# Sixteen activation rows per tensor, moved from a 1280-byte pitch to pitches of 1264 and 1272 bytes

## The reference

```
mod = silu(c) @ w_ada + b_ada                      # shift, scale, gate, twice
h   = rmsnorm(x) * (1 + scale1) + shift1
qa, ka, va, qb, kb, vb, r, glr = split(h @ w_in)   # 2048 -> 6160
oa  = attention, 16 heads of 64, three dilations, shared bias
ob  = gated linear attention, 4 heads, dk 128, dv 256
x   = x + gate1 * (concat(norm(oa), norm(ob) * silu(r)) @ w_out)
h2  = rmsnorm(x) * (1 + scale2) + shift2
g, u = split(h2 @ w_up)                            # 2048 -> 2 * 5632
x   = x + gate2 * ((silu(causal_conv3(g)) * u) @ w_down)
```

## Time and profile before

| | |
|---|---|
| median of 3 runs | 1544.93 us (1543.18 to 1546.24) |
| the profiled execution's span | 1544.0 us |
| mean granted TensorE clock | 0.993 of 2.4 GHz |
| busy: TensorE matmuls, weight loads | 98%, 89% |
| busy: VectorE, ScalarE, GpSimd | 57%, 41%, 3% |
| DMA | 371 MB, 240 GB/s on average |

### The profile page before, as it was taken

The page is one execution under the profiler, slowest core; times in us unless marked ns, Lnnn a source line. Parts: engine busy times, 40 slices in busy tenths (PEclk is TensorE's granted clock), DMA queues, the critical chain, the costliest instruction groups (busy, mean ns, idle before and its releaser), DMA issues.

```text
span 1544.0 us, 27862 instructions
## 1 busy us (share of the span) xinstructions
PE 1514.8 (98%) x11762; PEld 1372.8 (89%) x11762; DVE 875.7 (57%) x1509; ACT 633.9 (41%) x873; POOL 52.4 (3%) x89
## 2 busy tenths in 40 slices
PE   8999999999999889999999999999999999999999
PEld 4877888888888557768899999999999999999999
DVE  3655676666667435557454555555554565656574
ACT  3433444434445215235333333334333445545453
POOL 2000000001111000000000000000000000000000
PEclk8999999999999999999999999999999999999999
DMA  9998777777777997997644444454545444454541
GB/s 354 400 355 346 307 257 257 257 259 267 255 288 270 413 414 309 422 363 292 251 164 164 164 164 169 159 184 147 188 146 182 163 172 178 166 181 172 178 176 53
DMA packets 62283, 370.98 MB, mean 240 GB/s; under 512 B 7431, under 2 KB 7913, under 8 KB 27081
## 3 DMA queue, kind: packets, MB, share of 16 engines
q1 hardware_dynamic: 56096, 351.08, 60.6%
q0 software_dynamic: 5904, 17.93, 3.4%
q10 hardware_dynamic: 162, 0.22, 0.0%
HBM read 359.32 MB, written 9.88 MB: 239 GB/s over the span
## 4 chain that ended last, share of the span: by engine, by line
PE 89%; DMA 5%; DVE 3%; SPq 2%; ACT 1%; issue 1%; POOL 0%; ACTq 0%; DVEq 0%
PE ps L989 26%; PE ps L990 25%; PE ps L991 25%; PE ps L941 4%; PE ps L934 1%; SPq L710 1%; DMA ring<-in_w_ada_early 1%; DMA ring<-in_w_out 1%; DMA ring<-in_cache_k_win 1%; DMA proj<-in_tables 1%; ACT whi L1501 1%; DVE wlo L2028 1%; PE ps L1321 1%; DMA ring<-in_w_ada 1%; PE ps L1290 1%
## 5 line engine op out<-in xcount | busy, mean ns | idle before, releaser
L989 PE MATMUL ps<-hhi,whi 128*128 128x288 f32 x3136 | 934.0, 298 | 3.1 <-DVE wlo L1871 1.6
L990 PE MATMUL ps<-hlo,whi 128*128 128x288 f32 x3136 | 922.6, 294 | 0.0
L991 PE MATMUL ps<-hhi,wlo 128*128 128x288 f32 x3136 | 922.5, 294 | 0.0
L989 PEld LDWEIGHTS ps<-hhi,whi 128*128 128x128 f32 x3136 | 589.0, 188 | 38.8 <-issue 29.9
L990 PEld LDWEIGHTS ps<-hlo,whi 128*128 128x128 f32 x3136 | 589.2, 188 | 0.7
L991 PEld LDWEIGHTS ps<-hhi,wlo 128*128 128x128 f32 x3136 | 588.9, 188 | 0.0
L1492 ACT ACTIVATE whi<-ring 128x1024 fp32r<-128x1024 f32 x178 | 185.7, 1060 | 200.7 <-PE ps L991 200.7
L1864 DVE TENSOR_TENSOR wlo<-ring,whi 128x1024 fp32r<-128x1024 f32 x178 | 212.0, 1221 | 78.8 <-ACT whi L1492 78.4
L2028 DVE TENSOR_TENSOR wlo<-ring,whi 128x1024 fp32r<-128x1024 f32 x96 | 117.0, 1223 | 79.6 <-ACT whi L1501 79.5
L1501 ACT ACTIVATE whi<-ring 128x1024 fp32r<-128x1024 f32 x96 | 100.8, 1053 | 130.1 <-PE ps L991 114.2
L2545 DVE TENSOR_TENSOR wlo<-ring,whi 128x1024 fp32r<-128x1024 f32 (+1 forms) x94 | 105.7, 1132 | 56.2 <-ACT whi L1805 56.2
(11 more groups left out here) (298 smaller groups left out, 905.4 us busy)
## 6 DMA issues: line engine op xcount, KB each, us to landing
ring<-in_w_up SPq DMA_DIRECT2D x88, 1024.0 KB, 4.8
ring<-in_w_down SPq DMA_DIRECT2D x32, 1408.0 KB, 6.1
ring<-in_w_ada SPq DMA_DIRECT2D x42, 1024.0 KB, 6.8
ring<-in_w_in SPq DMA_DIRECT2D x28, 1024.0 KB, 6.5
ring<-in_w_ada_early SPq DMA_DIRECT2D x22, 1024.0 KB, 7.5
proj<-in_w_ada SPq DMA_DIRECT2D x22, 1024.0 KB, 11.0
ring<-in_w_in_early SPq DMA_DIRECT2D x20, 1024.0 KB, 9.3
ring<-in_w_out SPq DMA_DIRECT2D x16, 1024.0 KB, 13.2
```

The lines of the kernel that those rows point to most:

```text
L989: mm(out, w_hi, x_hi, start=start, stop=False)
L990: mm(out, w_hi, x_lo, start=False, stop=False)
L991: return mm(out, w_lo, x_hi, start=False, stop=stop)
```

## The change

The rows of `hhi` and `hlo` are addressed through a new helper, which builds a view with a given first column and a given pitch over the flat tensor. The tensors keep their size and place.

```
+def staggered(rows, first, pitch):
+
+    v = rows[:, first:first + TOK]
+    return bass.AP(v.tensor, v.offset, [list(v.ap[0]), [pitch, KD], [1, TOK]])
```

```
-            hhi = sbr("hhi", [P, KD, ROW], parts)[:, :, 0:TOK]
-            hlo = sbr("hlo", [P, KD, ROW], parts)[:, :, 0:TOK]
+            hhi = staggered(sbr("hhi", [P, KD * ROW], parts), 32, 316)
+            hlo = staggered(sbr("hlo", [P, KD * ROW], parts), 16, 318)
```

## The result

The changed kernel takes 1550.20 us (median of 6, 1549.93 to 1551.66) against 1544.16 us before (median of 6, 1542.72 to 1546.24), a ratio of 1.0042 with a 95% interval of 1.0032 to 1.0052. The medians differ by 6.0 us; the profiled execution has a span of 1548.6 us, 4.6 us more than the profiled one before.

What follows compares the result with a forecast made beforehand. The prediction took TensorE's distance of 0.1316 us from matmul to matmul to bound the kernel, certainly after 700 us. Its terms summed 0 + 0 + 0, giving 1545 us, with 1528 to 1582 us for 8 in 10.

Steps and rivals of the forecast that it cites:

- What bounds the kernel: From 700 us to the end everything trails TensorE, whose matmuls start 0.1316 us apart; earlier not quite so.
- The unit of account: 1 ns per matmul is 9.4 us over the kernel, of which 6.3 us, after 700 us, is certain to show.
- (a): ScalarE's and VectorE's writes of the rows and VectorE's reads of `hhi`: taken as 0, any difference hidden by slack.
- (b): TensorE's weight loads: `whi` and `wlo` do not move, so the effect was taken as 0.
- (c): TensorE's 9408 reads of the moving rows: all of any effect is here; taken as 0, both ends kept for the range.
- the measurement's bound: The least a measurement of this kernel can tell: about 0.2%, 3.1 us, which is 0.33 ns per matmul.
- The likeliest case: No measurable change in the whole kernel: 1545 us, own range 1542 to 1548, chance 0.47.
- rival A: Moving reads, lines 989 to 991: starts inside a block need one more; 1561 to 1565 us at 32 bytes; chance 0.28.
- smallest form: Sixteen-byte blocks: only the odd rows of `hlo` pay for one more block, 1568 matmuls x 1.8 ns = 2.8 us.
- The Trainium skill's rule: Each crossing to a new 16-byte line costs something; one more per moving row, 0.13 ns x 1568 = 0.2 us.
- Rival B: Weight load and moving read wait when meeting in the same memory part; other starts meet less: 1511 to 1538 us, chance 0.23.

Runs made afterwards that it cites:

- all_128: Kernel before with all 32 rows starting at 128 modulo 256 bytes, at the old pitch of 1280 bytes, weights unmoved; 1557.53 us, ratio 1.0088.
- all_8: Kernel before with all 32 rows starting at 8 modulo 256 bytes, pitch 320 columns; ratio 1.0142, 22.3 us slower.
- lo_only: The change with its lower rows alone (first column 16, pitch 318), upper rows again from column 0 at pitch 320; ratio 1.0024 to before.
- second scan: Kernel before with another placing of rows, weight slices or both in each of 42 units of w_up (96 matmuls each); 130.0 to 136.0 ns per matmul.
- both_16: The change with the lower rows placed like the upper ones (first column 32, pitch 316); ratio 1.0030 to before.
- first scan: Kernel before with moving rows read from other starts in 42 units of w_up, both parts alike or lower alone; 130.0 to 136.7 ns per matmul.
- the three scans: Kernel before with placings varied by w_up unit: row starts; rows and weights; then repeated and random placings, the random ones 131.1 to 135.5 ns.

## Why the prediction came out as it did

**What bounds the kernel** was right. Everything after 700 us follows TensorE's distance, and before 700 us nothing was lost at all: 1039 starts of line 996 by then, as before. The unit of account held too. Apart from the run with rows at 16, whose executions disagree, all versions came within what it gives, from 6291 to 9408 matmuls times the change in distance, but for the lower half alone: all_128 +1.7 ns, 10.7 to 16.0 us, measured 14.0 (1557.53 less 1543.50); all_8 +3.0 ns, 19 to 28, measured 22.3; rows at 144 -1.6 ns, 10 to 15 us less, measured 12.2; lo_only +0.3 ns, 1.9 to 2.8, measured 3.5 with an interval that reaches down to 2.3.

**Parts (a) and (b)**, the fills and the weight loads: right as far as the trace tells. The fills took 4 and 2 ns longer by the median, and 33 waits of `hhi` on TensorE stand ahead of them as before, 55.2 us for 54.4.

**Part (c), the moving reads, is the step that failed.** "I take 0" was wrong: it is 0.82 ns per matmul, 5.2 us in the part that shows, more than twice the measurement's bound of 0.33 ns. By the prediction's own sign (wrong if the starts per 100 us move by more than two while nothing else does) it was wrong: they moved by five. The likeliest case (1542 to 1548 us) missed the 1550.20. The wide range held it only because it was drawn up to 1582 us for rival A with blocks of 32 bytes, a mechanism that the runs exclude; that the time lies inside, and within half a per cent of the 1545, is luck as far as the mechanism goes. The reasoning leaned on three observations that could not carry it. The first, that the other engines and the DMA do not move the distance, is true and was confirmed row by row, but it says nothing on the two reads of TensorE itself. (Nor was the distance quite even: rows of 787 and 793 ns by turns, which the twelve matmuls of the earlier trace rows average away.) The second was that line 1112 runs at 128 modulo 256 and is not slow: there both the row and the weights are at 128, and the second scan shows that this is the same as both at 0 (131.7 ns); with the weights at 0 the same row costs 133.3. The row was near the new placement in its number and far from it in what counts. The prediction even named it, that both the load and the read side there have the offset, and took that as a point in favour. The third, the loads of line 1107 at 8 modulo 16, are weight loads for float32 transposes; they say nothing on a moving read, nor on how it stands to the load beside it.

**Rival A** had the right sign with the wrong mechanism. It gave 1561 us at the least, at blocks of 32 bytes, and the rows that are aligned do not keep their distance: row 8, where both parts start at 0, takes 792 ns for 787, and row 12 takes 799. Its smallest form, the odd rows of `hlo`, was sized at 1.8 ns on 1568 matmuls, 2.8 us if all of it showed. What both_16 against the change shows for the whole pattern of the lower rows is 132.4 less 132.0, 0.4 ns on each of the 9408, 2.7 us in the part after 700 us. The sizes are alike, but the loss is not the odd rows' alone, so the agreement is weak evidence for that form of A. Missing was the other half, the spreading itself.

**The Trainium skill's rule** on 16-byte lines (SBUF — State Buffer, the note on cachelines) gave 0.13 ns for a row that touches 73 lines in place of 72, an estimate as the prediction worked it out. It rests on the 9.1 ns above N / 2.4 + 2.5, the formula that the prediction took from the Trainium skill (TensorE: Matmul & The Clock Gate, section Back-to-back issue gap). The page gives that formula for the isolated gap of a single matmul, with no room in it for the weight loads that this stream has beside each one. So the 9.1 ns need not be the price of crossings at all. With all rows at 8 modulo 256 a matmul takes 2.8 ns more (first scan), some twenty times the 0.13. The measurement decides: one more crossing is not what such a placing costs. Nor is a start inside a line dear by itself, since the lower rows alone at 8 had 131.8 ns. The Trainium skill (SBUF — State Buffer, section Who interferes with whom) counts the moving and the weight reads as two independent ports; here the distance from start to start depends on how the two addresses stand to each other (131.7 ns with rows and weights both at 128, 133.3 with either alone there), so in this fp32r stream they are not independent in time.

**Rival B** had the ingredient, the weight load beside the read, and the wrong sign. It supposed that a common start is the worst relation and that any spreading helps. The table says that a common start (131.7) is better than the mean of the sixteen (132.4), and that one particular distance (144 bytes) is better by 1.7 ns. B's estimate of 1525 to 1538 us for a part of the waiting gone is where rows at 144 landed, 1531.83. That the waiting comes from meeting in the same part of the memory was not shown; only the dependence on the distance was.

**What the change does in one sentence:** it gives up a place that is better than average for a spread over all sixteen (half of the loss by the count of starts), and it gives the lower rows a pattern of their own, which costs as much again; whether by the starts in the middle of 16 bytes or by where the lower rows then stand is open.

## What to carry to other kernels

When a stream of matmuls keeps its distance whatever the other engines do, look at how each operand's start stands to the other's modulo 256 bytes, and measure the sixteen places before choosing; spreading the starts buys about the mean of the table, not its best entry. Moving all rows to 8 modulo 256 was the worst placing of a whole kernel here (+22.3 us), so prefer multiples of 16 bytes unless a measurement says otherwise. A row of the profile in which both operands sit at a new address is no evidence for moving only one of them, and a scan that gives each unit of one kernel its own placing measures forty of them in one execution; repeat some, since a unit can fall into a slower rhythm.

## What was not expected of the hardware

- Two rhythms for the same addresses, 130.0 and 131.1 ns, each held as long as the stream ran on: in the run with rows at 16 and weights at 128 it was 130.0 from 719 us up to an interruption at 788 us and 131.1 from there on. By the times, which one rules may differ from execution to execution (1529.93 against 1535.68 to 1538.77 us of one kernel).
- Of the 126 units of the three scans 85 lie within 0.05 ns of 130.0, 131.1, 131.7, 132.2 or 133.3 ns: few values for many placings. That the two reads lock to each other would explain it, but is not shown. What sets these values stays open; no placing tried went below 130.0 ns.
- Moving rows and weights together by 32, 64, 96, 128 or 192 bytes changes nothing (131.7 ns); moving them together by 16, 144 or 240 does (133.3, 130.6, 130.7). Why was not tried further.
